# Moving 40 scratch writes of each layer from SyncE's queue to GpSimd's, and one wait of SyncE to a later gate tile

## The reference

```python
sc = jnp.einsum('nhpd,hpkd->nhpk', q, sub_keys, preferred_element_type=jnp.float32)
sv, si = lax.top_k(sc, PEER_TOPK)
cand = sv[:, :, 0, :, None] + sv[:, :, 1, None, :]
...
gate = jax.nn.softmax(fv, axis=-1)
act = jax.nn.gelu(jnp.einsum('nd,nhed->nhe', xb, uu).astype(jnp.float32), approximate=False)
return jnp.einsum('nhe,nhed->nd', (gate * act).astype(xb.dtype), vv)
```

## Time and profile before

| | us |
|---|---|
| median of 3 runs | 3334.96 |
| lowest and highest | 3331.36, 3341.47 |
| profiled execution | 3339.47 |
| its span, first to last instruction | 3337.6 |
| PE busy | 3179.7 (95%) |
| DVE busy | 2674.1 (80%) |
| ACT busy | 1398.4 (42%) |
| POOL busy | 1213.5 (36%) |

### The profile page before, as it was taken

One profiled execution on the slowest core, in us unless ns is written; L12 is line 12 of the kernel. 1 busy time (PEld: TensorE's weight loads), 2 busy tenths in 40 slices (PEclk: granted clock), 3 DMA queues, 4 the chain that ended last, 5 costly groups with the idle time before them and its releaser, 6 DMA issues.

```text
span 3337.6 us, 48952 instructions
## 1 busy us (share of the span) xinstructions
PE 3179.7 (95%) x18217; PEld 2898.2 (87%) x18217; DVE 2674.1 (80%) x5383; ACT 1398.4 (42%) x2317; POOL 1213.5 (36%) x778
## 2 busy tenths in 40 slices
PE   8899898999999999999989989999989999999999
PEld 7788898998888888888879578989988888888888
DVE  6546389888788888888868937998878888888887
ACT  4553324777333333333333232277843333333332
POOL 2121322000455455555542033300025555555554
PEclk9897999999999999999999989999999999999999
DMA  3121222555999999999952332245579999999997
GB/s 127 50 64 50 93 79 89 209 195 197 342 374 368 359 369 356 363 368 359 365 176 70 12 84 64 93 154 206 209 278 379 367 370 360 367 357 363 368 358 268
DMA packets 425212, 807.82 MB, mean 242 GB/s; under 512 B 234176, under 2 KB 259328, under 8 KB 421504
## 3 DMA queue, kind: packets, MB, share of 16 engines
q1 hardware_dynamic: 317920, 444.73, 39.7%
q0 software_dynamic: 94560, 344.45, 27.9%
q10 hardware_dynamic: 12496, 15.51, 2.1%
HBM read 729.52 MB, written 76.08 MB: 241 GB/s over the span
## 4 chain that ended last, share of the span: by engine, by line
PE 80%; DVE 14%; ACT 2%; DMA 2%; issue 2%; POOL 0%; ACTq 0%; SPq 0%; DVEq 0%
PE bank L933 31%; PE bank L921 28%; PE bank L672 11%; PE bank L902 5%; DVE cv L2104 4%; DMA gt<-gate_matrix 1%; PE bank L814 1%; PE bank L859 1%; DVE oh L1745 1%; PE bank L659 1%; PE bank L830 1%; DVE oh L1740 1%; DVE hl L1529 0%; DVE root L1518 0%; DVE hQ L2008 0%
## 5 line engine op out<-in xcount | busy, mean ns | idle before, releaser
L921 PE MATMUL bank<-hh,ring 128*128 128x384 f32 x4096 | 1090.5, 339 | 21.7 <-ACT ga L1186 21.7
L933 PE MATMUL bank<-ring,wh 128*128 128x512 f32 x3072 | 831.4, 392 | 11.5 <-DVE wl L1772 11.5
L2161 POOL DMA_INDIRECT rows<-in_utab,gidx x320 | 447.4, 1398 | 994.9 <-DVE gidx L1686 590.2
L921 PEld LDWEIGHTS bank<-hh,ring 128*128 128x128 f32 x4096 | 744.9, 189 | 30.5 <-issue 22.2
L1754 DVE TENSOR_TENSOR ring<-raw,ring 128x1024 fp32r<-128x1024 f32 x494 | 602.4, 1223 | 206.1 <-ACT ring L1093 205.5
L1093 ACT ACTIVATE ring<-raw 128x1024 fp32r<-128x1024 f32 x598 | 622.5, 1052 | 198.9 <-PE bank L921 88.4
L921 PE MATMUL bank<-hl,ring 128*128 128x384 f32 x2048 | 687.6, 336 | 0.0
L933 PEld LDWEIGHTS bank<-ring,wh 128*128 128x128 f32 x3072 | 576.5, 188 | 123.9 <-DVE ring L1754 12.1
L2161 POOL DMA_INDIRECT rows<-in_vtab,gidx x320 | 492.2, 1538 | 367.4 <-DVE acc L1794 314.6
L672 PE MATMUL bank<-hh,ring 128*128 128x272 f32 x2752 | 495.1, 299 | 54.3 <-DVE hl L1529 47.7
L1186 ACT ACTIVATE ga<-bank 128x384 f32<-128x384 f32 x256 | 124.5, 486 | 961.9 <-PE bank L921 959.6
(11 more groups left out here) (318 smaller groups left out, 2876.7 us busy)
## 6 DMA issues: line engine op xcount, KB each, us to landing
raw<-in_stream SPq DMA_DIRECT2D x342, 512.0 KB, 5.7
raw<-in_vtab SPq DMA_DIRECT2D x256, 512.0 KB, 7.9
gt<-gate_matrix SPq DMA_DIRECT2D x256, 192.0 KB, 9.6
gate_matrix<-stage SPq DMA_DIRECT2D x20, 2048.0 KB, 9.9
units_ahead<-ga SPq DMA_DIRECT2D x96, 192.0 KB, 4.0
gv<-units_ahead SPq DMA_DIRECT2D x96, 192.0 KB, 8.7
gate_matrix<-stage ACTq DMA_DIRECT2D x4, 2048.0 KB, 9.2
rows<-in_utab,gidx POOLq DMA_INDIRECT x320, 8.0
```

The costliest lines, as they stand in the source:

```text
L921: m = T.matmul(unit_bank(e), w[:, ring_slot(t), k * P:(k + 1) * P], h[:, k, 0:ND], start=(k == 0 and i == 0), stop=(k == KC - 1 and i == 2))
L933: m = T.matmul(psum[c][:, a, :], w[:, v_n % WSLOT, c * P:(c + 1) * P], v[:, ring_slot(t), 512 * a:512 * a + 512], start=(v_n == 0 and i == ...
L2161: nc.gpsimd.indirect_dma_start(out=rows[:, g % ROW_SLOTS, :], out_offset=None, in_=vtab if is_v else utab, in_offset=bass.IndirectOffsetOn ...
```

## The change

SP no longer writes units 0 to 39 of either layer; POOL does, through its own queue and under semaphores of its own (`s_pwr`). POOL's remainders of tiles 4 to 8 alternate with the writes of units 0 to 4, and the other 35 writes stand between the last remainder and the first gathered row. SP keeps the writes of units 40 to 47. Every reader of a unit's write waits on the semaphore of the engine that issued it. At step 46 SP waits for `s_gw[0]` only; the wait for `s_gw[1]` moves to the gate tile of key 64.

```diff
+POOL_WRITES = 40
...
+        def unit_written(l, e):
+
+            mine = [x for x in range(AHEAD) if x % ASLOT == e % ASLOT and (x < POOL_WRITES) == (e < POOL_WRITES)]
+            s = s_pwr if e < POOL_WRITES else s_asp
+            return s[e % ASLOT], 16 * (len(mine) * l + mine.index(e) + 1)
...
             def load_gate(l, v):
                 e = V_ORDER[v]
+                if e == 64:
+                    sp.wait_ge(s_gw[1], 16 * (ND // 64) * (l + 1))
...
-                    sp.wait_ge(s_asp[e % ASLOT], 16 * ((AHEAD // ASLOT) * l + e // ASLOT + 1))
+                    sp.wait_ge(*unit_written(l, e))
...
                         sp.wait_ge(s_gi, 2 * (l + 1))
-                        for b in range(2):
-                            sp.wait_ge(s_gw[b], 16 * (ND // 64) * (l + 1))
+                        sp.wait_ge(s_gw[0], 16 * (ND // 64) * (l + 1))
...
-                    if 1 <= i <= AHEAD:
+                    if POOL_WRITES < i <= AHEAD:
                         write_units(l, i - 1)
...
-                    elif e >= ASLOT or l:
-                        act.wait_ge(s_asp[e % ASLOT], 16 * ((AHEAD // ASLOT) * l + n))
+                    elif e >= ASLOT:
+                        act.wait_ge(*unit_written(l, e - ASLOT))
+                    elif l:
+                        act.wait_ge(*unit_written(l - 1, e + AHEAD - ASLOT))
...
+            def write_units(l, e):
+                pool.wait_ge(s_ga, NKEY * l + e + 1)
+                pool.dma_start(adram[l, e], ga[:, e % ASLOT, :]).then_inc(s_pwr[e % ASLOT], 16)
+
+            def front_units(l):
+
+                for j in range(4, POOL_FRONT):
+                    lo(T_EXP[l] + j, ring_slot(T_EXP[l] + j), raw_buffer(T_EXP[l] + j))
+                    write_units(l, j - 4)
+                for e in range(POOL_FRONT - 4, POOL_WRITES):
+                    write_units(l, e)
...
-            lo_run(T_WQ[0], T_WQ[0] + N_WQ + POOL_FRONT)
+            lo_run(T_WQ[0], T_WQ[0] + N_WQ + 4)
+            front_units(0)
             gather_rows(0)
```

More of the change, by code:

```diff
@@ L398, in build @@
         s_asp = [sem(f"units{i}_written") for i in range(ASLOT)]
+        s_pwr = [sem(f"units{i}_written_by_pool") for i in range(ASLOT)]
         s_ald = [sem(f"units{i}_loaded") for i in range(ASLOT)]
@@ L1180, in gelu @@
                     act.wait_ge(s_used, t0 + POS_U[e] + 1)
-                    n = e // ASLOT
                     if e >= AHEAD + ASLOT:
                         act.wait_ge(s_wl, b_e + V_SEQ[e - ASLOT] + 1)
-                    elif e >= ASLOT or l:
-                        act.wait_ge(s_asp[e % ASLOT], 16 * ((AHEAD // ASLOT) * l + n))
+                    elif e >= ASLOT:
+                        act.wait_ge(*unit_written(l, e - ASLOT))
+                    elif l:
+                        act.wait_ge(*unit_written(l - 1, e + AHEAD - ASLOT))
                     A.activation(ga[:, e % ASLOT, :], unit_bank(e), ACT.Gelu).then_inc(s_ga, 1)
@@ L2208, in _ @@
             pool.dma_start(keys[:, :, :], keysT[1]).then_inc(s_keys, 16)
-            lo_run(T_WQ[1], T_WQ[1] + N_WQ + POOL_FRONT)
+            lo_run(T_WQ[1], T_WQ[1] + N_WQ + 4)
+            front_units(1)
             gather_rows(1)
```

## The result

| | before | after |
|---|---|---|
| median of 7 runs, us | 3334.96 (3331.36 to 3341.47) | 3345.13 (3339.64 to 3349.89) |
| ratio, 95% interval | | 1.0029 [1.0019, 1.0039] |
| span of the profiled execution, us | 3337.6 | 3348.1 |
| ACT's stage copy waits for gate writes, us | 2.0 | 8.4 |
| from `gelu(0)` to `gelu(48)`, layer 0 / 1, us | 321.1 / 319.1 | 325.4 / 324.5 |

The time lies inside the predicted range and 10.2 us above the predicted 3335. The interval excludes a ratio of 1, and it lies on both sides of the 0.3% that the prediction took as its bound. So the question of this study is where 10 us come from, when every term of the sum was 0.

A forecast was written before the change was run, and what follows sets the result against it. The prediction took PE, busy 95% of the span, to bound the kernel, so only its gaps could be won. Every term was 0, so it forecast the old median, 3335 us, with a range of 3322 to 3347.

The forecast's parts named there:

- rival B: Fronts of both layers: POOL's issues block DVE operations, slower, up to 3389 us, taken as 18 us more, 3353; chance 0.10.
- forecast of nothing measurable: Whole kernel: the change does nothing measurable, through whatever mix of earlier loads and shifted waits, median 3335 us; chance 0.78.
- Part 1: Step 46, both layers: SP no longer waits for the second gate write; the row numbers release it later anyway: 0.
- What SP loses: Fronts: SP sheds 40 issues a layer of about 0.33 us and gelu waits; earlier loads meet busy engines: 0.
- What POOL gains: Fronts: POOL gets 40 issues a layer of 0.75 us, 30 us a layer, fitting its idle time: 0.
- When the writes land: Fronts: unit e must land before gelu(e + 3); 0.75 + 3.4 us needed of 10.6, 6 us over: 0.
- Rival A: Change-over: second gate tile comes 7 us earlier and PE's stall goes, together 16.8 us faster, 3318; chance 0.12.
- the sum: Whole kernel: 0 for every part, so the median of before is kept, 3335 us.
- Q: Theory of the follow-up runs: in their own queue, POOL's unit writes go beside the gate writes, which land later; ratio 1.003.

The follow-up runs named there:

- e1: The kernel before with only the wait for the second gate write moved from step 46 to key 64, all unit writes left with SP: 3335.51 us, ratio 1.0002.
- e3: The changed kernel, but POOL waits for a gate write's landing before the first unit write behind it (units 11, 17, 24, 30, 37): 3337.46 us, ratio 1.0011.
- e5: The changed kernel with each of units 0 to 39 written a second time by POOL, to a tensor nobody reads: ratio 1.0035.
- e7: The changed kernel with only the three unit writes behind each gate write on POOL, 15 a layer, the other 25 on SP: ratio 1.0028.
- e9: The changed kernel with the three unit writes behind each gate write back on SP, the other 25 a layer on POOL: ratio 1.0004.
- e8: The kernel before with the second gate tile (key 48) loaded at step 46 right behind the first: ratio 1.0012.
- e10: The kernel before with the second gate tile loaded at step 46 behind the first gate tile and its unit: ratio 1.0016.

## Why the prediction was right, and where it failed

The time is inside the stated range, but only by the part of it that was reached for rival B. The forecast's own range was 3330 to 3342, and 3345.13 lies above it. It was widened to 3347 halfway towards B, and B did not occur. So the range held by luck, and the forecast of nothing measurable (0.78) did not: the interval excludes 1. (The lower end, 3322, is not halfway into A either: from 3330 to 3318 that is 3324. Nothing hangs on it.)

**Part 1** held: the moved wait is worth 0 (e1, 1.0002), for the reason given, the row numbers release SP.

**What SP loses** held in the main: by e3 the earlier loads have at most 1.3 us of the later landings. Most loads of layer 0's front are hardly earlier at all, since the wait for the remainder takes over: in 545 to 815 us SP now waits 207.2 us for remainders and 8.5 for a gelu, for 100.2 and 97.6 in the earlier trace rows.

```profile
SPq L476 <- DVE ring L1764: 207.2, 36, 17.1
...
SPq L487 <- ACT ga L1196: 8.5, 1, 8.5
```

**What POOL gains** held with a smaller price: 0.54 us for an issue, not 0.75. Rival B is out: DVE's one-hots take 342 ns at the median, for 344 in the earlier trace rows (a few reach 454 where the longest was 356), DVE's busy time in the two fronts is 555.3 us for 555.5, and twice the issues cost nothing that can be measured (e5). POOL's writes in layer 0's front, and their landings:

```profile
L2178 POOL DMA_DIRECT2D units_ahead<-ga x40: 540/540/587, 529.7 to 793.6; - x40
...
DMA to landing us min/median/max: 2.1/3.7/10.7
```

By the Trainium skill, SBUF — State Buffer, section "SBUF: two separate sides", a unit write could have been late by a whole DVE operation. No issue here took over 0.587 us, with DVE busy 88% of the stretch of the earlier trace rows. Whether one of DVE's operations beside them ran in such a mode, no row tells. **When the writes land** held as far as it went: in the changed kernel no gelu waits for a unit write. **Rival A** did not occur; the 2 us that PE stands less at layer 0's change-over in the profiled execution are no gain of the change, since e1 has them too at 1.0002.

**The step that failed** is the sum, by a term that it lacked. The paragraph on the landings asked only whether a unit write lands in time for those who wait for it. It did not ask whom the write passes. SP's queue had been an order between transfers: a unit write issued behind a gate write went behind it, as the 12.6 us of the earlier trace rows show, which the prediction itself read as "the slow ones presumably behind gate writes in the same queue". Taken out of that queue, the same 192 KB go beside the gate write. And the victim stood in the rows too: ACT's 0.9 us for a gate write in the earlier trace rows was the only wait on a transfer in that front, so the only sign of a transfer without slack. The missing term, by the numbers at hand: two or three units of 0.52 us (192 KB at 376 GB/s) for each of five gate writes in each of two layers, 10 to 16 us in all where every landing is waited for. Measured were 12.1 us of later landings, 6.4 of them in ACT's waits, and 9.7 us of longer fronts, of which PE stood 5.6 and ran slower at a lower granted clock for 4.1. The second share is missing from this estimate too, so that its agreement with the 10.2 us of time is in part chance. Of the theories, Q is shown by e3, e7 and e9: the unit writes that can pass a gate write are the cause. How the queues share the engines is not: e5 doubled the bytes without doubling the delay.

## What to carry to other kernels

A queue was here also an order between its transfers. Before small writes are moved to an idle engine, look for a large transfer that they stood behind, and for anyone who waits for it, even for 0.9 us; the free issue slots are not the whole price. Count a stall of PE at more than its length, since its clock may be lower behind it. If the move is wanted, hold the few writes that would pass it (e3), or leave just those in the old queue (e9: 25 of 40 writes moved at 1.0004).

At the change-over, where the stall is on a transfer, reordering only moved it (e8, e10).

## What the runs showed of the hardware that was not expected

- Twice the bytes in the second queue did not double the delay of the first: the ten landings grew by 1.3 us in sum (134.9 to 136.2), after 12.1 us for the first 192 KB of each unit. Not explained.
- Only the second half of a gate write pays: the ten first halves landed at 69.0 us in sum before and 68.8 after, the second halves at 122.8 and 134.9.
- A stall of 2.1 us on PE was followed by 3.5 us at a granted clock of 0.52, where the kernel before has 1.00; of the 9.7 us that the fronts grew, 4.1 are slower matmuls.
- POOL's direct transfer of 192 KB is issued in 0.54 us, one of 256 KB with another shape in 0.75.
